# The norm between two transformer blocks: two weight panels multiplied ahead of the norm's factor

## The chip, the core and the metric

The kernel runs on one core of one Trainium2 chip. A core has five engines that run their own instruction streams and meet only at semaphores: TensorE (matmuls, PE in the profile, its weight loads PEld), VectorE (DVE), ScalarE (ACT), GpSimd (POOL) and SyncE (SP, here the queue that loads the weights). The metric is the device time of one execution in microseconds (us). Matmul results land in PSUM, which has 8 banks of 128 partitions x 512 fp32 numbers; everything else lies in SBUF.

## What is computed

Two transformer blocks of two layers each, on 512 tokens of width 1024, in fp32. Between the blocks stands a norm over the width of each token:

```python
def rmsnorm(x, g):
    y = x * rsqrt(mean(x * x, axis=-1, keepdims=True) + EPS)
    return y * g

x = first_block(...)      # ends with  return rmsnorm(x, g_final)
x = second_block(x, ...)
```

The second block's first layer multiplies the normed stream by a wide `w_in` and uses two slices of the product, `iq` (512 columns) and `iw` (8 columns), only to choose keys:

```python
proj = x @ w_in
aq, ak, av, iq, ik, iw, ... = split(proj)
# per query t and key s, over 8 index heads h:
dots  = einsum('bqhd,bsd->bqhs', iq, ik) * 64 ** -0.5
score = einsum('bqhs,bqh->bqs', relu(dots), iw * 8 ** -0.5)
# the 128 best admissible keys of each query are attended to
```

The norm's factor of token t, 1/rms(t), is positive, so that it can be taken out of `iq` (and of the relu) and put on `iw` of the same token.

## The kernel before

**Layout.** The stream lies transposed, as `X[128, 8, 512]`: tile k holds 128 of the 1024 channels for all 512 tokens. Every fp32 product is made from three: a tile is split into a high part (`XH`, rounded) and a low part (`XL`, the rest), and `wh*xh + wh*xl + wl*xh` are added up in a PSUM bank. ACT makes high parts, DVE the low parts of the stream, POOL the low parts of the weights.

**Weights.** They come as 274 panels of 1 MB through two raw buffers (`RAW`), in the order of their use. ACT's `hi(c)` (line 1246) splits panel c's high half, POOL's `low_half` (line 342) its low half, and then SP loads panel c+2 into the same raw buffer (line 330). Two panels in a row can have buffers of their own (`own_place`, `OWN_H`, `OWN_L`), so that they are split while the panels before them are still in use. The two `iq` panels of the second block's first layer have them.

**Order on TensorE.** The first block's last work is the down projection of its feed-forward part, in 8 groups. DVE adds each 128x512 result to `X` (line 2236). Then `inverse_deviation` (line 719) adds the squares of all channels up by matmuls with ones, and, once ACT has taken the root of the 4x128 sums and DVE the reciprocal, `spread` (line 709) copies the factor of each token over 128 partitions of bank 5. `keep_clock` (line 669) issues matmuls whose results nobody reads. Then `gemm_two` (line 593) multiplies the two `iq` panels: for each k ("a row" below), 8 matmuls with `XH[k]` and 4 with `XL[k]` of 384 columns, into banks 0 to 3. Behind it stands `misc`, a panel that holds `ik`, `iw` and a few others, then the panels of `aq`, and so on.

**Order on ACT.** At the end of the feed-forward part (`next_panel`, line 1495) ACT first runs five steps of `beside`, which is empty in the last layer of the first block, then splits the two `iq` panels. Behind that come `norm` (line 1539): eight squares of `X` (line 1282), the root, the `misc` panel, and eight `split_hi` of the normed stream with the next panel's split between them.

**Order on DVE.** In the last group of the down projection, `down` (line 2230) puts one step of `adding` behind each added tile from the third on: the running sum of the squares (line 1961, six additions; the last square is added on TensorE). Behind that, `norm` (line 2016): the reciprocal, then for each k a `scalar_tensor_tensor` that multiplies `X[k]` by the gain and the spread factor, in place, and the subtraction that makes `XL[k]`.

**A place of the same kind.** The first block's second layer starts differently, through `entry(1)` (ACT line 1557, DVE line 1990): its first panel is multiplied with `X` times the gain alone, and the factor comes later. There ACT makes `XH[k]` (line 1566, "u_hi") and a square in turn, DVE makes `XL[k]` from X, gain and `XH[k]` (line 1997, "u_lo") and adds a square, and TensorE makes the sums by `token_sums` (line 656; eight matmuls of one column) behind a whole panel.

Of the kernel before, what the change touches and what calls it, by code (L numbers as in the profile page):

```python
# [15 lines left out]
F32 = mybir.dt.float32  # L16
F32R = mybir.dt.float32r
I32 = mybir.dt.int32
ALU = mybir.AluOpType
# [3 lines left out]
P = 128  # L23
D = 1024
S = 512
DEPTH = 2
# [200 lines left out]
def program(nc, stream, x_in, consts_in, rot_in, vec_in, wgate_in, pos_in, out, marks):  # L227
    ctx = ExitStack()
    with ctx:
# [282 lines left out]
        def _(pe):  # L512
# [205 lines left out]

            def inverse_deviation(bank, t, l, which):

                T.after((t, l, which + "_acc", KD - 2), bank_reader[bank], own=False)
                token_columns(TMP[:, 2, :], bank, P, True, False)
                T.after((t, l, which + "_sq", KD - 1), own=False)
                T.done(token_columns(TMP[:, (KD - 1) % 2, :], bank, P, False), t, l, which + "_ms")
                bank_reader[bank] = (t, l, which + "_root")
                keep_clock(bank + 1, 1)
                spread(bank + 1, (t, l, which + "_inverse"), (t, l, which + "_spread"))
                bank_reader[bank + 1] = (t, l, which + "_scaled", KD - 1)
                keep_clock(bank, 2)
# [353 lines left out]
            inverse_deviation(4, "f", 0, "n1")  # L1083

            for l in range(DEPTH):
# [4 lines left out]
                gemm_two(w["iq"], banks, h_ready, lambda k: (t, l, "x_hi", k), lambda m: (t, l, "q", 8 + m), columns_b(8))  # L1090
# [150 lines left out]
        def _(act):  # L1241
# [159 lines left out]
            def ffn(l, t, ff, groups, kt, base_t, base_d, base_h, beside=iter(())):  # L1401
# [108 lines left out]

# [22 lines left out]
            def token_root(bank, ready, name):  # L1533

                A.after(ready)
                sums = PS[:, bank, 0:S:P] if name[0] == "f" else PS[:, bank, 0:NB]
                A.done(act.activation(ST[:, 100:104], sums, ACT.Sqrt, scale=1.0 / D, bias=ST[:, 96:97]), *name)

            def norm(t, l, which, squared, bank, second_panel, to_x=False):

                for _ in squared:
                    pass
                warm_root()
                token_root(bank, (t, l, which + "_ms"), (t, l, which + "_root"))
                hi(second_panel, used=panel_used(second_panel - 4) if to_x else None)
                for k in range(KD):
                    if to_x and k == 4:
                        hi(second_panel + 1, used=panel_used(second_panel - 3))
                    src = X[:, k, :] if to_x else TMP[:, k % 2, :]
                    hn = ("b", 0, "x_hi", k) if to_x else (t, l, ("h_hi" if which == "n1" else "h2_hi"), k)  # L1550
                    split_hi(XH[:, k, :], src, [(t, l, which + "_scaled", k)], hn, own=False)

            def read_first(l):
                for m in range(2):
                    read(("a", l, "q", m), AR[:, m, :])

# [35 lines left out]
            entries = [entry(l) for l in range(DEPTH)]  # L1592
            for l in range(DEPTH):
# [126 lines left out]
                ffn(l, t, w["ff"], FF1_GROUPS, 4, *bases(t, l), entries[l + 1] if l + 1 < DEPTH else iter(()))  # L1720
            norm("f", 0, "n1", norm_squares("f", 0, "n1", lambda k: ("a", DEPTH - 1, "ffn_out", k)), 4,
                 at_b(0)["misc"], to_x=True)
# [207 lines left out]
        def _(dve):  # L1930
# [25 lines left out]
            def sums(src, ready, name):  # L1956

                for k in range(1, KD - 1 if name[0] == "f" else KD):
# [45 lines left out]

            def scale_again(t, l, gain):
# [9 lines left out]

            def norm(t, l, which, gain, to_x=False):
                token_inverse(t, l, which)
                h = "h" if which == "n1" else "h2"
                spread_bank = 7 if which == "n2" else 5

                def dst(k):
                    return X[:, k, :] if to_x else TMP[:, k % 2, :]

                def hi_name(k):
                    return ("b", 0, "x_hi", k) if to_x else (t, l, h + "_hi", k)

                def lo_name(k):
                    return ("b", 0, "x_lo", k) if to_x else (t, l, h + "_lo", k)

                gains = VEC[:, 1 if to_x else l % 2, gain:gain + KD]  # L2030
                for k in range(KD + 1):
                    if k < KD:

                        V.after(*[hi_name(k - 2), lo_name(k - 2)] if k >= 2 else [(t, l, which + "_spread")], own=False)
                        V.done(dve.scalar_tensor_tensor(dst(k), X[:, k, :], gains[:, k:k + 1], PS[:, spread_bank, :],
                                                        ALU.mult, ALU.mult), t, l, which + "_scaled", k)
                    if k:
                        j = k - 1
                        lo(XL[:, j, :], dst(j), XH[:, j, :], [hi_name(j)], lo_name(j), own=False)
# [230 lines left out]
            entries = [entry(l) for l in range(DEPTH)]  # L2270
            for l in range(DEPTH):
# [70 lines left out]
                ffn(l, t, FF1_GROUPS, 4, *bases(t, l), entries[l + 1] if l + 1 < DEPTH else square_sums("f", 0, "n1"))  # L2342
            norm("f", 0, "n1", VB["g_final"], to_x=True)

            for l in range(DEPTH):
# [13 lines left out]
                V.after()  # L2359
                V.done(dve.memset(AR[:, 13, 0:P], 1.0))  # L2360
# [197 lines left out]
```

How the kernel before makes its waits and increments, by code:

```python
    def after(self, *names, own=True):  # L205
        need = {}
        for name in names:
            if name is None or (name not in self.marks and not self.marks.get("complete")):
                continue
            who, n = self.marks[name]
            need[who] = max(need.get(who, 0), n)
        if own:
            need[self.name] = self.n
        for who, n in need.items():
            if n > 0:
                self.eng.wait_ge(self.sems[who], n)
# [65 lines left out]
        def const_dma(eng, dst, src, name):  # L283
            if n_consts[0]:
                eng.wait_ge(const_loaded, 16 * n_consts[0])
            eng.dma_start(dst, src).then_inc(const_loaded, 16)
            n_consts[0] += 1
            marks[name] = ("const", 16 * n_consts[0])
# [27 lines left out]
        @block.sync  # L317
# [6 lines left out]
            sp.dma_start(RAW[:, 1, :], stream[1:2, :, :].rearrange("o p n -> p (o n)")).then_inc(raw_full[1], 16)
            with sp.Fori(1, NPANELS // 2) as i:
                for s in range(2):
                    sp.wait_ge(lo_ready, 2 * i + s + 1)
                    sp.dma_start(RAW[:, s, :], stream[bass.ds(2 * i + s, 1), :, :].rearrange("o p n -> p (o n)"))\
                        .then_inc(raw_full[s], 16)
            for k in range(KD):
                sp.wait_ge(sems["act"], marks.get(("b", DEPTH - 1, "ln2_x", k), ("act", 1))[1])
                sp.dma_start(out.rearrange("(k p) s -> p k s", p=P)[:, k, :], X[:, k, :]).then_inc(stored, 16)
            sp.wait_ge(stored, 16 * KD)
```

## Time and profile before

| | |
|---|---|
| time, median of the runs | 3341.56 us |
| the profiled execution's own time | 3339.35 us |
| its span, first to last instruction | 3337.5 us |
| TensorE busy (PE) | 3301.5 us, 99% of the span |
| VectorE, ScalarE, GpSimd busy | 1567.9, 1370.2, 1470.4 us |
| TensorE's granted clock, mean over the span | 0.998 of full speed |
| DMA | 299 MB, 90 GB/s mean |

The profile is of one execution. Its span is what the instructions fill; 1.8 us of its own time lie around the span. Busy shares are means over a span in which the stages have different limits, so that the stretch of the changed work has to be read by itself, in the timeline.

### The profile page before, as it was taken

Reading aid. Unit: us, or ns where it says so; the run is one execution under the profiler, and the core shown is the slowest. Engines: PE = TensorE matmul, PEld = TensorE weight load, DVE = VectorE, ACT = ScalarE, POOL = GpSimd, SP = SyncE. Lnnn points to the kernel's source line nnn. Section 1 sums busy time; section 2 is a strip of 40 time slices with the busy share of each in tenths; the row PEclk is TensorE's granted clock in tenths of the full one; section 3 lists DMA queues with packets and bytes.
Section 4 is the critical chain, followed back from the end, with each engine's and each line's share of the span. In section 5 each row is a group of like instructions: output and inputs, shape, how many; then the busy total and the mean of one; then the engine's idle time right before and its main releaser. Section 6 shows DMA issues by size and latency. Waiting matters only on the chain. (4 is left out here: it accounts for less than half of the span.)

```text
span 3337.5 us, 45362 instructions
## 1 busy us (share of the span) xinstructions
PE 3301.5 (99%) x16670; PEld 2748.5 (82%) x16670; DVE 1567.9 (47%) x2488; ACT 1370.2 (41%) x1989; POOL 1470.4 (44%) x1102
## 2 busy tenths in 40 slices
PE   9999999999999999999999999999999999999998
PEld 7888888888788888888878888888887788888887
DVE  7523332226514442224973446544488625464445
ACT  5535332224635342223364453333343635443333
POOL 4433544445343444445433345445544233445453
PEclk9999999999999999999999999999999999999999
DMA  4222222222222322222211222222222121222221
GB/s 153 89 73 86 89 103 95 94 101 95 77 76 76 103 100 100 89 101 106 88 66 66 73 92 99 84 95 101 101 81 87 64 76 68 97 85 92 101 98 66
DMA packets 44014, 299.02 MB, mean 90 GB/s; under 512 B 4816, under 2 KB 5456, under 8 KB 8784
## 3 DMA queue, kind: packets, MB, share of 16 engines
q1 hardware_dynamic: 41696, 291.52, 24.5%
q10 hardware_dynamic: 2160, 5.33, 0.5%
q8 instruction: 107, 1.75, 0.2%
q14 instruction: 51, 0.42, 0.0%
HBM read 294.74 MB, written 2.10 MB: 89 GB/s over the span
## 5 line engine op out<-in xcount | busy, mean ns | idle before, releaser
L349 POOL TENSOR_TENSOR w_lo<-w_raw,w_hi 128x512 fp32r<-128x512 f32 x1024 | 1364.6, 1365 | 1778.2 <-ACT w_hi L1257 1778.2
L526 PE MATMUL ps<-x_hi,w_hi 128*128 128x512 f32 x2296 | 907.2, 395 | 3.1 <-DVE arena L2195 2.2
L528 PE MATMUL ps<-x_hi,w_lo 128*128 128x512 f32 x2296 | 894.8, 390 | 0.0
L527 PE MATMUL ps<-x_lo,w_hi 128*128 128x512 f32 x2296 | 894.1, 389 | 0.0
L1257 ACT ACTIVATE w_hi<-w_raw 128x1024 fp32r<-128x1024 f32 x516 | 515.9, 1049 | 463.0 <-PE ps L528 339.4
L526 PEld LDWEIGHTS ps<-x_hi,w_hi 128*128 128x128 f32 x2296 | 431.5, 188 | 100.3 <-issue 6.4
L528 PEld LDWEIGHTS ps<-x_hi,w_lo 128*128 128x128 f32 x2296 | 431.2, 188 | 91.2
L527 PEld LDWEIGHTS ps<-x_lo,w_hi 128*128 128x128 f32 x2296 | 431.6, 188 | 89.0 <-issue 2.2
L526 PE MATMUL ps<-y_hi,w_hi 128*128 128x512 f32 x1056 | 411.9, 390 | 2.2 <-issue 1.9
L528 PE MATMUL ps<-y_hi,w_lo 128*128 128x512 f32 x1056 | 410.9, 389 | 0.0
L527 PE MATMUL ps<-y_lo,w_hi 128*128 128x512 f32 x1056 | 410.8, 389 | 0.0
L2236 DVE TENSOR_TENSOR x<-x,ps 128x512 f32<-128x512 f32 x272 | 182.2, 684 | 255.5 <-PE ps L528 255.3
L2195 DVE SCALAR_TENSOR_TENSOR arena<-ps,vec,arena 128x511 f32<-128x511 f32 (+1 forms) x176 | 131.5, 749 | 300.4 <-ACT arena L1467 290.1
L526 PEld LDWEIGHTS ps<-y_hi,w_hi 128*128 128x128 f32 x1056 | 198.2, 188 | 45.1 <-issue 4.2
L527 PEld LDWEIGHTS ps<-y_lo,w_hi 128*128 128x128 f32 x1056 | 198.2, 188 | 41.5 <-issue 0.5
L528 PEld LDWEIGHTS ps<-y_hi,w_lo 128*128 128x128 f32 x1056 | 198.2, 188 | 41.3
L632 PE MATMUL ps<-w_hi,x_hi 128*128 128x256 f32 x768 | 222.2, 289 | 1.2 <-POOL w_lo L349 1.2
L633 PE MATMUL ps<-w_hi,x_lo 128*128 128x256 f32 x768 | 217.1, 283 | 0.0
L634 PE MATMUL ps<-w_lo,x_hi 128*128 128x256 f32 x768 | 217.1, 283 | 0.0
L1273 ACT ACTIVATE arena<-ps 128x512 f32<-128x512 f32 x136 | 81.3, 598 | 315.8 <-PE ps L528 240.6
L1467 ACT ACTIVATE arena<-ps,vec 128x512 f32<-128x512 f32 x88 | 68.4, 779 | 277.4 <-PE ps L528 277.4
L2206 DVE SCALAR_TENSOR_TENSOR arena<-ps,tmp 128x512 f32<-128x512 f32 x64 | 44.0, 691 | 238.5 <-PE ps L528 224.9
(269 smaller groups left out, 4178.7 us busy)
## 6 DMA issues: line engine op xcount, KB each, us to landing
w_raw<-stream SPq DMA_DIRECT2D x274, 1024.0 KB, 4.8
x<-x_t SPq DMA_DIRECT2D x4, 512.0 KB, 8.1
rotary<-rot ACTq DMA_DIRECT2D x4, 512.0 KB, 4.0
y_t<-x SPq DMA_DIRECT2D x8, 256.0 KB, 2.1
ct<-consts ACTq DMA_DIRECT2D x2, 770.0 KB, 4.4
arena<-pos ACTq DMA_DIRECT2D x2, 256.0 KB, 2.6
w_gate<-w_gate_in ACTq DMA_DIRECT2D x2, 256.0 KB, 2.8
vec<-vectors ACTq DMA_DIRECT2D x4, 116.0 KB, 2.0
```

The source lines that it names most:

```text
L349: ins = nc.gpsimd.tensor_tensor(low(c)[:, o:o + S], RAW[:, c % 2, o:o + S], high(c)[:, o:o + S].bitcast(F32), ALU.subtract)
L526: pe.matmul(ps, wh, xh, start=(k == 0), stop=False)
L527: pe.matmul(ps, wh, xl, start=False, stop=False)
L528: return pe.matmul(ps, wl, xh, start=False, stop=last)
L632: pe.matmul(ps, xh, wh, start=(k == 0), stop=False)
L633: pe.matmul(ps, xl, wh, start=False, stop=False)
L634: mm = pe.matmul(ps, xh, wl, start=False, stop=(k == KD - 1))
L1257: act.activation(wh[:, o:o + 2 * S], RAW[:, s, o:o + 2 * S], ACT.Copy)\
L1273: A.done(act.activation(dst, bank_of(*name), func, **kw), *(("read",) + name))
L1467: act.activation(AR[:, j, :], PS[:, j, :], ACT.Identity, scale=VEC[:, l % 2, bass.ds(tap, 1)], bias=VEC[:, l % 2, bass.ds(bias, 1)]).then_ ...
L2195: ins = dve.scalar_tensor_tensor(AR[:, j, tap:S], PS[:, j, 0:n], wv, AR[:, j, tap:S], ALU.mult, ALU.add)
L2236: dve.tensor_tensor(X[:, m, :], X[:, m, :], PS[:, 4 + m % 4, :], ALU.add).then_inc(down_added, 1)
```

## The change

The two `iq` panels of the second block's first layer are multiplied with `X` times `g_final`, without the factor. The factor goes on `iw`. The last layer of the first block gets an `entry` of its own (`last_entry`), in which ACT makes high parts and squares in turn while the feed-forward part ends, and DVE the low parts; both `iq` panels are split ahead of these. TensorE runs two of the eight rows, then `token_sums` (now of all eight squares, which DVE adds up), a third row, `spread`, and the last five rows. `inverse_deviation` goes, and with it two calls of `keep_clock` (12 matmul instructions of 256 columns in the profile) and 16 of 128 columns. The stream is then multiplied by gain and factor as before, but each `XH[k]` is overwritten only when row k has been read, which TensorE says by a new mark.

```diff
-            def gemm_two(n, banks, ready, high_ready, name, columns):
+            def gemm_two_rows(n, banks, ready, high_ready, name, columns, read=None):
 ...
                         if k == KD - 1:
                             T.done(mm, *name(j))
+                        elif read and j == 3:
+                            T.done(mm, *read(k))
+                    if k < KD - 1:
+                        yield
...
-            inverse_deviation(4, "f", 0, "n1")
...
-                gemm_two(w["iq"], banks, h_ready, lambda k: (t, l, "x_hi", k), lambda m: (t, l, "q", 8 + m), columns_b(8))
+                if l:
+                    gemm_two(w["iq"], banks, h_ready, lambda k: (t, l, "x_hi", k), lambda m: (t, l, "q", 8 + m), columns_b(8))
+                else:
+                    index = gemm_two_rows(w["iq"], banks, lambda k: ("f", 0, "u_lo", k), lambda k: ("f", 0, "u_hi", k),
+                                          lambda m: (t, l, "q", 8 + m), columns_b(8), lambda k: ("f", 0, "u_read", k))
+                    run(index, 2)
+                    token_sums(TMP[:, 2, :], 4, ("f", 0, "n1_acc", KD - 1), ("f", 0, "n1_ms"))
+                    bank_reader[4] = ("f", 0, "n1_root")
+                    run(index)
+                    spread(5, ("f", 0, "n1_inverse"), ("f", 0, "n1_spread"))
+                    bank_reader[5] = ("f", 0, "n1_scaled", KD - 1)
+                    for _ in index:
+                        pass
...
                     else:
-                        run(beside, 5)
+                        if ff + per * groups not in own_place:
+                            run(beside, 5)
                         hi(ff + per * groups)
                         if ff + per * groups in own_place:
                             hi(ff + per * groups + 1)
+                            run(beside, 5)
...
+            def last_entry():
+                x_ready = lambda k: ("a", DEPTH - 1, "ffn_out", k)
+                squared = norm_squares("f", 0, "n1", x_ready)
+                for k in range(KD):
+                    A.after(x_ready(k), "vec%d" % (DEPTH - 1))
+                    g = VB["g_final"] + k
+                    A.done(act.activation(XH[:, k, :], X[:, k, :], ACT.Copy, scale=VEC[:, 1, g:g + 1]), "f", 0, "u_hi", k)
+                    yield
+                    if k < 6:
+                        run(squared)
+                        yield
+                for _ in squared:
+                    pass
+                warm_root()
+                token_root(4, ("f", 0, "n1_ms"), ("f", 0, "n1_root"))
...
+            misc = at_b(0)["misc"]
+            hi(misc, used=panel_used(misc - 4))
+            for k in range(KD):
+                if k == 4:
+                    hi(misc + 1, used=panel_used(misc - 3))
+                split_hi(XH[:, k, :], X[:, k, :], [("f", 0, "n1_scaled", k), ("f", 0, "u_read", k)], ("b", 0, "x_hi", k), own=False)
...
+            def last_entry():
+                adding = square_sums("f", 0, "n1")
+                for k in range(KD):
+                    g = VB["g_final"] + k
+                    V.after(("f", 0, "u_hi", k), "vec%d" % (DEPTH - 1), own=False)
+                    V.done(dve.scalar_tensor_tensor(XL[:, k, :], X[:, k, :], VEC[:, 1, g:g + 1],
+                                                    XH[:, k, :].bitcast(F32), ALU.mult, ALU.subtract), "f", 0, "u_lo", k)
+                    if k:
+                        run(adding)
+                    yield
+                for _ in adding:
+                    pass
...
+                if l == 0:
+                    V.done(dve.tensor_tensor(iw, iw, ST[:, 104:108].unsqueeze(2).broadcast_to([P, NB, 8]), ALU.mult))
+                    V.after()
```

The first `last_entry` shown is that of ACT, the second that of DVE. `scale_stream` on DVE holds the loop that `norm` held, without a change in its instructions.

## Rows read from the trace of the kernel before

**Rows 1.** The page, part 1: busy time, share of the span, instructions of each engine
```profile
PE 3301.5 (99%) x16670; PEld 2748.5 (82%) x16670; DVE 1567.9 (47%) x2488; ACT 1370.2 (41%) x1989; POOL 1470.4 (44%) x1102
```
**Rows 2.** Timeline, TensorE, around the norm: start us, us, engine, line, instruction, count
```profile
1550.28 0.39 PE L528 MATMUL ps<-y_hi,w_lo 128*128 128x512 f32 x1
1552.05 2.05 PE L679 MATMUL ps<-ct,tmp 128*128 128x128 f32 x16 [1.38 <-DVE tmp L1961]
...
1557.47 0.41 PE L531 MATMUL ps<-x_hi,own_hi 128*128 128x384 f32 x1
...
1559.63 0.33 PE L531 MATMUL ps<-x_hi,own_hi 128*128 128x384 f32 x1
...
1561.71 0.33 PE L531 MATMUL ps<-x_hi,own_hi 128*128 128x384 f32 x1
...
1574.46 0.47 PE L526 MATMUL ps<-x_hi,w_hi 128*128 128x512 f32 x1
```
**Rows 3.** Timeline, ScalarE, the same stretch
```profile
1530.92 1.99 ACT L1257 ACTIVATE own_hi<-w_raw 128x1024 fp32r<-128x1024 f32 x2
1540.11 2.01 ACT L1257 ACTIVATE own_hi<-w_raw 128x1024 fp32r<-128x1024 f32 x2 [7.21 <-DMA w_raw<-stream]
1542.03 1.34 ACT L1282 ACTIVATE tmp<-x 128x512 f32<-128x512 f32 x2
```
**Rows 4.** Timeline, GpSimd, the same stretch
```profile
1541.25 5.96 POOL L349 TENSOR_TENSOR own_lo<-w_raw,own_hi 128x512 fp32r<-128x512 f32 x4 [1.05 <-ACT own_hi L1257]
```
**Rows 5.** Timeline, VectorE, around the norm and at the end of the key selection
```profile
1537.10 0.69 DVE L2236 TENSOR_TENSOR x<-x,ps 128x512 f32<-128x512 f32 x1 [2.03 <-PE ps L528]
...
1551.31 0.68 DVE L1961 TENSOR_TENSOR tmp<-tmp 128x512 f32<-128x512 f32 x1
...
1691.05 0.29 DVE L2055 CUSTOM_DVE_ANT_0 tmp<-arena,ps 128x128 f32<-128x128 f32 x1 [4.42 <-PE ps L746]
```
**Rows 6.** Timeline, VectorE and ScalarE, entry(1) of the first block
```profile
774.19 1.18 DVE L1997 SCALAR_TENSOR_TENSOR x_lo<-x,vec,x_hi 128x512 fp32r<-128x512 f32 x1
775.48 1.60 DVE L1961 TENSOR_TENSOR tmp<-tmp 128x512 f32<-128x512 f32 x1
...
780.10 0.75 DVE L1997 SCALAR_TENSOR_TENSOR x_lo<-x,vec,x_hi 128x512 fp32r<-128x512 f32 x1
780.95 0.69 DVE L1961 TENSOR_TENSOR tmp<-tmp 128x512 f32<-128x512 f32 x1
781.56 0.68 DVE L2236 TENSOR_TENSOR x<-x,ps 128x512 f32<-128x512 f32 x1
782.16 0.74 DVE L1997 SCALAR_TENSOR_TENSOR x_lo<-x,vec,x_hi 128x512 fp32r<-128x512 f32 x1
...
774.50 0.73 ACT L1566 ACTIVATE x_hi<-x,vec 128x512 fp32r<-128x512 f32 x1
```
**Rows 7.** Timeline, TensorE, entry(1): the sums and the spread between rows of a panel
```profile
792.16 0.95 PE L660 MATMUL ps<-ct,tmp 128*128 128x1 f32 x8
792.97 0.49 PE L531 MATMUL ps<-x_hi,w_hi 128*128 128x512 f32 x1
...
795.84 1.05 PE L715 MATMUL ps<-ct,stats 128*128 128x128 f32 x8
796.64 0.48 PE L531 MATMUL ps<-x_hi,w_hi 128*128 128x512 f32 x1
```
**Rows 8.** Timeline, TensorE, an idle stretch in an attention and the matmuls behind it
```profile
832.99 1.12 PE L746 MATMUL ps<-arena 64*128 64x128 f32 x8 [2.06 <-DVE stats L2055]
834.04 0.79 PE L526 MATMUL ps<-x_hi,w_hi 128*128 128x512 f32 x1
...
836.75 0.40 PE L526 MATMUL ps<-x_hi,w_hi 128*128 128x512 f32 x1
```
**Rows 9.** Stretches: length, busy time of PE, PEld, DVE, ACT, POOL, granted clock, DMA
```profile
834.00:836.00 2.00, 2.00 (x6) 1.57 (x6) 1.32 (x9) 1.89 (x8) 1.09 (x1) 0.50 0.23 92
68.00:70.00 2.00, 0.00 (x0) 0.00 (x0) 1.79 (x10) 0.99 (x1) 0.00 (x0) 1.00 0.86 344
```

More of the change, by code:

```diff
@@ L591, in gemm_rows, with gemm_two @@
                 marks[("panel", n)] = marks[name(ms - 1)]
-            def gemm_two(n, banks, ready, high_ready, name, columns):
+            def gemm_two(*args):
+                for _ in gemm_two_rows(*args):
+                    pass
+            def gemm_two_rows(n, banks, ready, high_ready, name, columns, read=None):
                 for p in range(2):
@@ L717, in spread @@
                 T.done(mm, *name)
[L719 to L729, printed above, removed]
             def attention(pairs, l, t, fillers, ahead=0):
@@ L1089, in _ @@
                 banks = range(4) if l == 0 else range(4, 8)
-                gemm_two(w["iq"], banks, h_ready, lambda k: (t, l, "x_hi", k), lambda m: (t, l, "q", 8 + m), columns_b(8))
+                if l:
[11 more added lines that the diff above has]
+                        pass
+                    marks[("f", 0, "u_read", KD - 1)] = marks[(t, l, "q", 11)]
                 gemm(w["misc"], KD, 1, XH, XL, h_ready, lambda m: (t, l, "q", 12))
@@ L1535, in token_root, with read_first @@
                 A.after(ready)
-                sums = PS[:, bank, 0:S:P] if name[0] == "f" else PS[:, bank, 0:NB]
+                sums = PS[:, bank, 0:NB]
                 A.done(act.activation(ST[:, 100:104], sums, ACT.Sqrt, scale=1.0 / D, bias=ST[:, 96:97]), *name)
-            def norm(t, l, which, squared, bank, second_panel, to_x=False):
+            def read_first(l):
+                for m in range(2):
+                    read(("a", l, "q", m), AR[:, m, :])
+            def last_entry():
[9 more added lines that the diff above has]
+                        yield
                 for _ in squared:
@@ L1543, in norm @@
                 warm_root()
[L1544 to L1555, printed above, removed]
+                token_root(4, ("f", 0, "n1_ms"), ("f", 0, "n1_root"))
             def entry(l):
@@ L1591, in _ @@
             hi(0)
-            entries = [entry(l) for l in range(DEPTH)]
+            entries = [entry(l) for l in range(DEPTH)] + [last_entry()]
             for l in range(DEPTH):
@@ L1719, in _ @@
                     const_dma(act, VEC[:, 0, :], vec_in[2], "vec2")
-                ffn(l, t, w["ff"], FF1_GROUPS, 4, *bases(t, l), entries[l + 1] if l + 1 < DEPTH else iter(()))
-            norm("f", 0, "n1", norm_squares("f", 0, "n1", lambda k: ("a", DEPTH - 1, "ffn_out", k)), 4,
-                 at_b(0)["misc"], to_x=True)
+                ffn(l, t, w["ff"], FF1_GROUPS, 4, *bases(t, l), entries[l + 1])
+            for _ in entries[DEPTH]:
+                pass
[5 more added lines that the diff above has]
+                split_hi(XH[:, k, :], X[:, k, :], [("f", 0, "n1_scaled", k), ("f", 0, "u_read", k)], ("b", 0, "x_hi", k), own=False)
             const_dma(act, VEC[:, 1, :], vec_in[3], "vec3")
@@ L1956, in sums @@
             def sums(src, ready, name):
-                for k in range(1, KD - 1 if name[0] == "f" else KD):
+                for k in range(1, KD):
                     a = src(0) if k == 1 else TMP[:, 2, :]
@@ L2003, in entry, with scale_stream @@
                     pass
+            def last_entry():
[9 more added lines that the diff above has]
+                for _ in adding:
+                    pass
+            def scale_stream(gain):
+                for k in range(KD + 1):
+                    if k < KD:
+                        V.after(("f", 0, "n1_spread"), own=False)
+                        V.done(dve.scalar_tensor_tensor(X[:, k, :], X[:, k, :], VEC[:, 1, gain + k:gain + k + 1],
+                                                        PS[:, 5, :], ALU.mult, ALU.mult), "f", 0, "n1_scaled", k)
+                    if k:
+                        j = k - 1
+                        lo(XL[:, j, :], X[:, j, :], XH[:, j, :], [("b", 0, "x_hi", j)], ("b", 0, "x_lo", j), own=False)
             def scale_again(t, l, gain):
@@ L2014, in scale_again @@
                         lo(XL[:, j, :], TMP[:, j % 2, :], XH[:, j, :], [(t, l, "h_hi", j)], (t, l, "h_lo", j), own=False)
[L2016 to L2039, printed above, removed]
             def attention(pairs, l, t, beside):
@@ L2268, in ffn @@
                     pass
-            entries = [entry(l) for l in range(DEPTH)]
+            entries = [entry(l) for l in range(DEPTH)] + [last_entry()]
             for l in range(DEPTH):
@@ L2341, in _ @@
                 token_inverse(t, l, "n2")
-                ffn(l, t, FF1_GROUPS, 4, *bases(t, l), entries[l + 1] if l + 1 < DEPTH else square_sums("f", 0, "n1"))
-            norm("f", 0, "n1", VB["g_final"], to_x=True)
+                ffn(l, t, FF1_GROUPS, 4, *bases(t, l), entries[l + 1])
+            for _ in entries[DEPTH]:
+                pass
+            token_inverse("f", 0, "n1")
+            scale_stream(VB["g_final"])
             for l in range(DEPTH):
```

## The prediction

> **What bounds the kernel now.** Read the page's first part first: TensorE is busy 99% of the span [rows 1], so an edit can only win what TensorE loses at one place, and only if TensorE doesn't lose it again beside it. Then the timeline of TensorE around the norm [rows 2]. The last matmul of the feed-forward part starts at 1550.28. A row of the index panels, 12 matmuls of 384 columns, takes 1561.71 - 1559.63 = 2.08 us, 0.173 each, so a matmul of 512 columns takes 0.173 x 512/384 = 0.23, and TensorE is free for the next block at 1550.51. The first index matmul starts at 1557.47. Between lie 6.96 us of a wait for the sum of squares, sums, idle-time matmuls and spread. The index panels then take eight rows, 16.6 us, and `misc` starts at 1574.46; 0.35 us of these 16.99 are start and turnover. Everything that the change touches on TensorE lies between 1550.51 and 1574.46: 23.95 us. I read `misc`'s start as the goal post.
>
> Then the timelines of ScalarE, GpSimd and VectorE in the same stretch, to see when the inputs of the new order are there. ScalarE splits the first index panel at 1530.92, waits 7.21 us for the second's data, splits it from 1540.11 and is free for the stream at 1542.03 [rows 3]. GpSimd is at that panel's low half from 1541.25 to 1547.21 [rows 4]. Both panels are thus ready before 1550.51, and the first three tiles of the stream are final by 1537.10 + 0.69 [rows 5].
>
> **The change part by part.** *Rows 0 and 1 ahead of the sums.* They need u_hi and u_lo of two tiles, made from 1542.03 on, and start at 1550.51 without a wait: to 1550.51 + 2 x 2.08 = 1554.67.
>
> *The sum of squares.* This is the term that decides. `token_sums` stands behind row 1 and waits for the seventh addition, and this chain is now VectorE's whole work: u_lo of eight tiles, seven additions and the last five tiles of the stream, one behind the other. It can't start before the first u_hi, and ScalarE comes to that only behind the second panel: 1542.03 + 0.73 [rows 3, 6] and a semaphore's 0.1, so 1542.85. The steps from start to start are in entry(1) [rows 6]: u_lo to addition 0.85, addition to stream tile 0.61, stream tile to u_lo 0.60, together 2.06. u_lo 0 to the stream's tile takes 0.65; five such triples 10.3; then two pairs without a stream tile, 0.85 + 0.61 each, 2.92; and 0.08 to the end of the last: 13.95. ScalarE's u_hi and square take 1.6 us a pair with their waits [rows 3, 6] and hold u_lo 1 up by 0.3. That gives 1557.1 if nothing slows VectorE. But GpSimd works beside it until 1547.21 or a little longer, and in entry(1) beside GpSimd a u_lo took 1.18 instead of 0.75 and an addition 1.60 instead of 0.69 [rows 6]. Two u_lo and one addition fall in that time: 0.43 + 0.43 + 0.91, less part of the 0.3, gives 1558.6. If the third u_lo is caught as well, and by as much as the addition was (0.91), 1559.5. Ends: 1557.1 and 1559.5. I take 1558.5, near the middle one, whose rows are of the same instructions beside the same engine. Before, the last addition on VectorE ended at 1551.99 [rows 5], with none of the low parts in the chain.
>
> The Trainium skill (SBUF — State Buffer, "Who interferes with whom") says that a VectorE instruction with two SBUF inputs and a GpSimd instruction that reads SBUF lock each other out, one waiting for the whole of the other. Rows 6 agree with it in kind, 1.60 against 0.69. By it every such instruction up to 1547.2 could wait for one whole GpSimd instruction, a quarter of the 5.96 us [rows 4], and the chain would end about 1 us later than the upper end.
>
> *The new wait.* TensorE stands still from 1554.67 to 1558.55, 3.9 us. What is queued behind it is all its work. The removed wait was 1.38 us long [rows 2] and the matmuls around it filled the rest; nothing fills this one.
>
> *The small matmuls.* `token_sums` takes 792.97 - 792.16 = 0.81, `spread` 796.64 - 795.84 = 0.80 [rows 7], each with 0.1 for the slower first matmul behind it. The factor (root, reciprocal) is covered by row 2, 2.08 us.
>
> *The sum.* 1550.51 + 4.16 (rows 0, 1) + 3.9 (wait) + 0.9 (sums) + 2.08 (row 2) + 0.9 (spread) + 10.4 (rows 3 to 7) = 1572.85; with the turnover of 0.3, `misc` starts at 1573.1 instead of 1574.46: 1.4 us less, 2.8 at the chain's early end, 0.4 at its late end.
>
> *The clock.* Where TensorE stood idle for 2.06 us before 832.99 [rows 8], the granted clock fell: 0.50 in 834 to 836 [rows 9], which is 1.2 instead of 2.4 GHz. The six matmuls from 834.04 took 2.71 us to 836.75 instead of 6 x 0.23 = 1.4: the fall cost 1.3. In another place TensorE was idle all through 68 to 70 and kept 1.00 [rows 9]. So an idle stretch of 2 to 3 us may or may not bring the fall; 3.9 us are longer than both, and the dummy matmuls that stood here are gone. I take a fall as likely, three in four, and its price as 1.0, below the 1.3 because part of the slow time passes over the wait and over `token_sums`, which are not limited by the clock.
>
> The Trainium skill (TensorE: Matmul & The Clock Gate, "HAM oscillation — how this bites in real kernels") warns of this pattern: TensorE that idles between groups of matmuls starts each group cold. It speaks against the change; by it the sum is -0.4, by the row at 68 to 70 alone -1.4.
>
> *Moved and added work that I cost at nothing.* `misc` is split behind the root as before, but some 5 us later, at about 1560; with 5.96 us on GpSimd [rows 4] it is ready near 1567, 5 us ahead of its use, and SP's load of the panel behind it waits for this too, with as much room. The overwriting of each `XH[k]` waits for its row; only tile 7 is late: its high and low part, 0.73 + 0.75 and two waits, against 7 x 3 x 0.23 = 4.8 us that `misc` spends on the first seven tiles. The multiplication of `iw` is smaller than a stream tile's 0.68 [rows 6], and reading the index results moves behind the last high part: together VectorE is up to 2 us later against TensorE than before. VectorE comes to the end of the key selection 4.42 us before TensorE gives it work [rows 5], which covers it; without that cover it would cost those 2 us. The removed square on TensorE and the keep-clock matmuls are in the 6.96.
>
> **The sum against the runs.** The working is that of one execution, 3339.35 us (span 3337.5 and 1.8 around it). The median of the runs is 3341.56, 2.2 above. I take the difference off the median: -1.4 + 1.0 = -0.4, 3341.2.
>
> **The rivals.** *Forecast:* the wait moves to the sum of squares, 3.9 us, and the clock falls once: 3341.2, chance 0.5. Its own range is 3340.2 to 3342.2, by the chain's two ends.
> *The clock stays.* The wait is there, TensorE goes on at 2.4 GHz. For it: 68 to 70. Against it: 832.99. It gives -1.4, 3340.2; at the chain's early end -2.8, 3338.8. Chance 0.25.
> *Slower: the slow clock lasts.* Behind the wait come one-column sums, a single row, and `spread`; if these don't bring the clock back, it stays at 1.2 GHz for twice the work of rows 8 and costs 2.6. -1.4 + 2.6 = +1.2, 3342.8, and with the chain's late end 3343.8. Against it: at 832.99 the clock was back after one stretch. It decides from the point where the clock costs more than 1.4. Chance 0.18.
> *The wait goes for good.* If the sums came in time for row 1, no wait would be left: 6.96 - 0.9 - 0.9 = 5.2 less, 3336.4. The chain would have to end by 1554.67; it starts at 1542.85 and needs 13.95 us of VectorE. Chance 0.04.
> The rest, 0.03, is for what I haven't seen.
>
> **How the numbers follow.** The range holds the first three: 3338.8 to 3343.6. Faster or slower by over 2% would be 67 us, about what a measurement of this kernel can tell from no change; no case comes near: faster 0.005, same 0.985, slower 0.01.
>
> **What would show it.** Right: index matmuls from 1550.5 on without a gap behind the feed-forward part; TensorE idle for about 3.9 us before the one-column matmuls, released by VectorE's addition; rows below 1.00 of granted clock within some us of it; `misc` at 1573 to 1574. Wrong: no wait before `token_sums`; an addition chain that ends before 1557; a wait in `misc` for a low part or a panel; or VectorE not idle any more before the attention at 1691.

## The result and the profile after

The changed kernel takes 3349.5 us (median), the kernel before 3341.18: 1.0024 times as long, 95% interval 1.0016 to 1.0032, some 8 us more. It lies outside the predicted 3338.8 to 3343.6, and the interval lies wholly above 1: the change makes the kernel slower, by a quarter of a percent. One of the ten runs of the kernel before took 7672.95 us and the others 3340.89 to 3343.34; without it the median is 3341.15.

The first page of the profile doesn't show it. TensorE is busy for 3302.8 us, 3301.5 before [rows 1]; its mean clock is 0.996, 0.998 before. The 8 us have to be looked for in the stretch itself. One caution first: the feed-forward part ahead of the norm ended between 1550.4 and 1553.6 in the profiled executions, and it moved without any edit ahead of it as well (1550.51 in the kernel before, 1552.11 in e8, which is the same kernel up to there; 1552.13 after the change). So all places below are counted from the end of that part, called E.

The timeline of TensorE after the change, around the norm (start, us, engine, line, instruction):

```profile
1560.71 1.87 PE L668 MATMUL ps<-ct,tmp 128*128 128x1 f32 x8 [4.23 <-DVE tmp L1979]
1562.44 0.67 PE L531 MATMUL ps<-x_hi,own_hi 128*128 128x384 f32 x1
...
1566.02 1.05 PE L723 MATMUL ps<-ct,stats 128*128 128x128 f32 x8
1566.83 0.42 PE L531 MATMUL ps<-x_hi,own_hi 128*128 128x384 f32 x1
...
1581.63 0.47 PE L526 MATMUL ps<-x_hi,w_hi 128*128 128x512 f32 x1 [4.14 <-issue]
...
1583.52 0.63 PE L526 MATMUL ps<-x_hi,w_hi 128*128 128x512 f32 x1
1583.95 0.63 PE L527 MATMUL ps<-x_lo,w_hi 128*128 128x512 f32 x1
```

The stretches of the two falls of the clock (length, busy time of PE, PEld, DVE, ACT, POOL, granted clock, DMA):

```profile
1560.00:1566.00 6.00, 5.29 (x20) 5.29 (x21) 0.84 (x2) 2.15 (x3) 2.10 (x2) 0.54 0.00 0
1582.00:1586.00 4.00, 4.00 (x12) 3.14 (x11) 3.71 (x8) 1.10 (x3) 0.00 (x0) 0.57 0.53 215
```

These lines answer to rows 2, 7 and 8. Two rows of the index panels follow the feed-forward part without a gap. Then TensorE waits for the sum of squares, 4.23 us by the profile, which counts the tail of the last matmul as busy, and 4.42 from the end of two rows' time (1552.13 + 2 x 2.08 = 1556.29) to 1560.71. The sums take 1562.44 - 1560.71 = 1.73 us and row 2 takes 1566.02 - 1562.44 = 3.58 at a granted clock of 0.54, which is 1.2 GHz for nearly all of it. The last rows run at full speed, and `misc` stands still for 4.14 us more. The releaser of that wait is given as "issue": the profile names nobody. Behind it the clock is down again, 0.43 us from matmul to matmul instead of 0.23. `misc` starts 29.50 us behind E, 23.95 before [rows 2].

Who keeps `misc` waiting stands in ScalarE's timeline (ACTq are DMA issues):

```profile
1578.61 0.63 ACT L1284 ACTIVATE x_hi<-x 128x512 fp32r<-128x512 f32 x1 [1.07 <-DVE x L2042]
1578.62 0.34 ACTq L287 DMA_DIRECT2D vec<-vectors  x1
1580.60 0.33 ACTq L287 DMA_DIRECT2D w_gate<-w_gate_in  x1
1581.04 1.66 ACT L1767 ACTIVATE arena<-ps 128x384 f32<-128x384 f32 x3 [1.80 <-DMA vec<-vectors]
```

`misc` is summed in bank 0. Bank 0 holds the first index result, and ScalarE reads it (L1767) only behind the last high part of the stream and behind two small loads, the second of which waits for the first (`const_dma` waits for the load ahead of it). The first read is done at about 1581.6; `misc` starts at 1581.63. Before, the index results were read as soon as they were there, because ScalarE was through with the stream by then and stood waiting for TensorE:

```profile
1573.87 2.25 ACT L1749 ACTIVATE arena<-ps 128x384 f32<-128x384 f32 x4 [5.60 <-PE ps L609]
```

### The profile page after: what moved, and what is told of

The parts are those of the page before. It is cut to its first block and busy times, and to the rows that moved or that the text cites. A ratio compares the mean times of both kernels' runs of the same rounds, so it can differ in the third digit from the quotient of the medians.

```text
span 3346.9 us, 45359 instructions
## 1 busy us (share of the span) xinstructions
PE 3302.8 (99%) x16650; PEld 2749.6 (82%) x16650; DVE 1576.3 (47%) x2498; ACT 1376.2 (41%) x1997; POOL 1468.9 (44%) x1102
## 3 DMA queue, kind: packets, MB, share of 16 engines
q8 instruction: 107, 1.75, 0.2%
```

## The experiments

The terms E, "misc" and "score matmuls" (the products of `iq` and `ik`, line 1107 before, 1114 after, 1120 where the bank is edited) are as above. Theory A, B and so on are named in the expectations. Eleven kernels ran (there is no e6), each beside the kernel before on the same chip; ratios are to that. An interval is about 3 us either way, so that the times alone don't rank e1 to e7, and a difference of 1 or 2 us between two medians is not shown by them. What is said below of single microseconds rests on places in the timelines, of one profiled execution each.

**e1: the two small loads behind misc's read.**

```diff
-            const_dma(act, VEC[:, 1, :], vec_in[3], "vec3")
...
-                const_dma(act, WG[:, :], wgate_in[l], ("w_gate", l))
+                if l:
+                    const_dma(act, WG[:, :], wgate_in[l], ("w_gate", l))
...
                                    "read", t, l, "q", j)
+                            if l == 0:
+                                const_dma(act, VEC[:, 1, :], vec_in[3], "vec3")
+                                const_dma(act, WG[:, :], wgate_in[l], ("w_gate", l))
```

> The two small loads that ScalarE issues between the last high part of the stream and the reads of the index results (the next layer's vectors and the gate weights) are issued only behind the misc panel's read. Theory A (the wait of 4.1 us ahead of misc is for misc's PSUM bank, bank 0, which still holds an index result that ScalarE reads late): the read starts 1.8 us earlier, at the end of the last high part, so misc's wait falls from 4.1 to about 2.3 us and the time by 1.8 us, to about 3347.7. Theory B (misc waits for a low part of the stream or of its panel): the wait stays 4.1 and the time 3349.5. Theory C (only the slow clock costs): 3349.5 as long as the clock falls twice.

Measured: 3346.37, ratio 1.0015 (1.0006 to 1.0024). TensorE and ScalarE around `misc`, from their timelines:

```profile
1579.68 0.47 PE L526 MATMUL ps<-x_hi,w_hi 128*128 128x512 f32 x1 [2.39 <-POOL w_lo L349]
...
1578.37 0.63 ACT L1284 ACTIVATE x_hi<-x 128x512 fp32r<-128x512 f32 x1 [1.07 <-DVE x L2045]
1579.09 2.25 ACT L1770 ACTIVATE arena<-ps 128x384 f32<-128x384 f32 x4
```

The wait falls by 1.75 us, as theory A says, and the clock doesn't fall in `misc` any more (granted 1.00 from 1580 to 1590). The medians differ by 3.1 us where 1.8 were expected; the second fall, which theory A left out, was 1.6 us in the changed kernel and fits the rest. (The profile now names GpSimd as the releaser; the low half of `misc`'s panel had been done at 1568.7.)

**e2: misc in a bank of its own.**

```diff
+                if l == 0:
+                    forced.append(4)
                 gemm(w["misc"], KD, 1, XH, XL, h_ready, lambda m: (t, l, "q", 12))
```

`next_bank` takes a bank from `forced`, where there is one, instead of the ring's next.

> misc is summed in PSUM bank 4, which is free since the root was taken, instead of bank 0. Theory A: misc starts right behind the index panels; its wait of 4.1 us goes, and with it the second fall of the clock (about 1.7 us): 3343.7. Theory B: the wait for a low part or a panel stays, 3349.5. Theory C (the clock alone): the second fall goes only if the wait goes, else 3349.5.

Measured: 3346.52, ratio 1.0015 (1.0006 to 1.0024). The wait is gone to the last bit: the last four index matmuls start at 1575.35 and take 4 x 0.173 us, and `misc` starts at 1576.04.

```profile
1575.35 0.85 PE L617 MATMUL ps<-x_lo,own_hi 128*128 128x384 f32 x4
1576.04 0.39 PE L530 MATMUL ps<-x_hi,w_hi 128*128 128x512 f32 x1
```

So theory A is right on whose wait it was, and B is out. But the time fell by 3.0 us only, not by 5.8. `misc` starts 24.56 us behind E; the attention, 140.0 behind E before, starts at 145.0. TensorE's waits from 1566 to 1692 tell where the gain went (who waited for whom: us in total, times, longest):

```profile
PE ps L1120 <- ACT tmp L1756: 2.6, 5, 1.1
PE ps L644 <- POOL w_lo L349: 1.0, 1, 1.0
```

Before, the score matmuls had no such wait. ScalarE copies their results into two buffers that VectorE empties, and ScalarE's own waits ahead of these copies are for VectorE (e.g. 3.91 us at 1619.80); so behind these waits stands VectorE.

**e3: four rows ahead of the sums.** In the order on TensorE, `run(index, 2)` becomes `run(index, 4)`.

> Four rows of the index panels run ahead of the one-column sums instead of two. Theory A: the first wait (4.2 us) goes, as two rows are 4.2 us of work, and the clock stays up; but the index results are still read by ScalarE behind the last high part, which hangs on VectorE's chain behind the spread; this moves earlier only by the time that the spread does (2.3 us), so misc starts about 2.3 us earlier, behind a longer wait (8 us instead of 4): 3347.2. Theory D (the first wait costs its full length and its fall of the clock): 4.2 + 2.3 = 6.5 us less, 3343.0.

Measured: 3346.72, ratio 1.0019 (1.0010 to 1.0028).

```profile
1558.94 1.05 PE L668 MATMUL ps<-ct,tmp 128*128 128x1 f32 x8
...
1578.22 0.76 PE L526 MATMUL ps<-x_hi,w_hi 128*128 128x512 f32 x1 [8.88 <-issue]
```

The wait ahead of the sums is gone, and `misc` now waits 8.88 us instead of 4.14. It starts 27.79 us behind E, 1.7 earlier than in the changed kernel, and the median is 2.8 less. That is near theory A (2.3); D's 6.5, a ratio of 1.0005, lies outside the interval. A wait taken away on TensorE was given back at the next place where TensorE meets the same chain.

**e4: matmuls nobody reads in both waits.**

```diff
+                    keep_clock(6, 4)
                     token_sums(TMP[:, 2, :], 4, ("f", 0, "n1_acc", KD - 1), ("f", 0, "n1_ms"))
...
                     marks[("f", 0, "u_read", KD - 1)] = marks[(t, l, "q", 11)]
+                    keep_clock(6, 4)
```

> Eight matmuls nobody reads are put in each of the two waits (ahead of the one-column sums and ahead of misc), into bank 6; the waits stay as long. Theory A: each fall of the clock costs, the first 0.9 us in the one-column sums and 1.4 us in the row behind, the second 1.7 us in misc; without them 3349.5 - 4.0 = 3345.5. Theory E (the clock is a bystander, the waits alone make the loss): 3349.5. The rest up to 3341.2 would be the waits themselves.

Measured: 3345.85, ratio 1.0014 (1.0005 to 1.0023). The granted clock by stretch (columns as above):

```profile
1557.00:1566.00 9.00, 8.34 (x50) 7.48 (x50) 4.64 (x9) 4.35 (x7) 1.96 (x2) 1.00 0.00 0
1580.00:1586.00 6.00, 5.01 (x22) 4.18 (x23) 4.56 (x10) 1.97 (x4) 0.00 (x0) 1.00 0.52 209
```

With both waits filled the clock stays at 1.00, the spread starts 11.59 us behind E instead of 13.89, `misc` 27.84 instead of 29.50, and the median is 3.7 us less; 4.0 were expected. TensorE still comes to `misc` too early and has nothing of use to do, for longer than before (4.95 us from its last index matmul, 4.31 in the changed kernel), since `misc` waits for ScalarE's read. So somewhat less than half of the change's loss is the clock, the rest the waits themselves. Theory E is out by these places; by the times alone it would not be, as the two intervals overlap.

**e5: four rows and the own bank together.**

> Both waits are taken away at once: four rows ahead of the one-column sums, and misc in bank 4. Theory G (TensorE's own order sets the time): rows, sums and misc follow each other without a wait, misc starts 18.8 us behind the feed-forward part instead of 23.95, and the time is 5 us under before: 3336. Theory F (VectorE sets the time: it is at work without a break from the sums of squares over the stream's parts and the rotations to the scores, and TensorE's score matmuls wait for it): VectorE comes to the first rotation 27.5 us behind the feed-forward part, 24.07 in before; less a slack of about 1.3 us that the score matmuls had, 2.1 us over before: 3343.3, with waits in the score matmuls.

Measured: 3345.31, ratio 1.0013 (1.0003 to 1.0022). `misc` starts 18.84 us behind E, as theory G has it, 5 us earlier than before. The time is 4.4 us over before all the same. TensorE's waits behind it:

```profile
PE ps L530 <- DVE x_lo L1963: 2.3, 3, 0.8
PE ps L1120 <- DVE stats L2384: 1.8, 1, 1.8
PE ps L644 <- POOL w_lo L349: 1.0, 1, 1.0
PE ps L1120 <- ACT tmp L1756: 0.9, 2, 0.6
```

TensorE runs ahead and waits for VectorE in `misc` (the stream's low parts), ahead of the scores (the index weights), and in them. Theory G is out: TensorE's own order doesn't set the time here.

**e7: the stream's first parts between the two panels' splits.** `run(beside, 5)` stands between the two `hi` of the index panels.

> The stream's first parts are made between the splits of the two index panels instead of behind both, in ScalarE's 7.2 us of waiting for the second panel's data; nothing else of the changed kernel is touched. The chain of squares starts when the stream's tiles come and ends about 5.3 us behind the feed-forward part instead of 8.5. Theory A+F: the first wait falls from 4.2 to 1.2 us, the clock stays up there, the spread comes 4.8 us earlier and with it VectorE and the read of the index results; misc starts 24.8 us behind the feed-forward part (29.5 in the changed kernel, 23.95 in before): 3342 to 3344, by whether the clock falls in the wait ahead of misc. Theory B (misc waits for its panel, which is split behind the root): about the same gain. Theory H (the order of the splits is what made the change slow by itself): 3341 or less.

Measured: 3344.34, ratio 1.0013 (1.0004 to 1.0023). The squares end 5.68 us behind E, 8.53 in the changed kernel; the first wait is 1.39 us. `misc` starts 25.06 behind E (24.8 expected), behind a wait of 4.77 us:

```profile
1557.55 1.05 PE L668 MATMUL ps<-ct,tmp 128*128 128x1 f32 x8 [1.39 <-DVE tmp L1979]
...
1576.87 0.76 PE L526 MATMUL ps<-x_hi,w_hi 128*128 128x512 f32 x1 [4.77 <-issue]
```

It recovers 5.2 us by the medians (3.7 by the ratios) and leaves `misc`'s wait and the clock's fall in it. The order "both panels first" is one part of the loss, not the whole: theory H asked for 3341 or less, which lies outside the interval. Whether it is the dearest part the ratios don't tell (1.0013 here, 1.0013 in e5, 1.0014 in e4).

**e8: VectorE made late in the kernel before.**

```diff
+                if l == 0:
+                    for _ in range(7):
+                        V.after()
+                        V.done(dve.tensor_tensor(YSCR[:, KD + 1, :], ROT[:, 0, :], ROT[:, 1, :], ALU.add))
                 for j in range(8, 13):
                     rope_b(j)
```

> The kernel before, with seven additions of 128x512 (about 0.75 us each with their waits, 5.3 us) put on VectorE ahead of the first rotation of the index results; their result is used by nothing. Theory F: the score matmuls have about 1.3 us of slack against VectorE, the rest becomes TensorE's wait: 4.0 us more, 3345.2, waits at the score matmuls. Theory I (as the prediction had it: VectorE's lateness is covered by its wait of 4.4 us ahead of the attention): 0.9 us more, 3342.1, no waits at the score matmuls.

Measured: 3340.68, ratio 0.9999 (0.9989 to 1.0008): nothing. But it tells nothing between the theories, because I had put the additions into an idle stretch. VectorE in e8, then its waits in the kernel before (1560 to 1692):

```profile
1571.88 5.05 DVE L2356 TENSOR_TENSOR scratch<-rotary 128x512 f32<-128x512 f32 x7
1577.04 0.01 DVE L1944 LOAD_MASK_SELECT scratch<-arena  x1
```
```profile
DVE scratch L1944 <- ACT arena L1749: 4.4, 1, 4.4
DVE tmp L2055 <- PE ps L746: 4.4, 1, 4.4
```

Before, VectorE waited 4.4 us for the first index result (L1944 is the rotation), and the additions filled that. The first rotation began 24.95 us behind E instead of 24.08. What the miss is worth: it shows VectorE's slack in front of the rotations, 4.4 us, which the change had to spend as well.

**e9: all together**: the order of e7, three rows ahead of the sums, misc in bank 4, the loads of e1.

> All together: the stream's first parts between the two splits, three rows ahead of the sums, misc in bank 4, the two small loads behind misc's read. Theory G: no wait from the feed-forward part to misc, 18.5 us instead of 23.95: 5.4 us under before, 3335.8. Theory F: VectorE comes to the first rotation 23.85 us behind the feed-forward part, 0.2 earlier than in before; with the slack of 1.3 us the gain is 1.5: 3339.7, and the rest of TensorE's lead is waited off at the score matmuls.

Measured: 3343.06, ratio 1.0002 (0.9993 to 1.0012). `misc` starts 18.47 us behind E without a wait (18.5 expected), the first rotation 24.22 behind E (23.85 expected). The score matmuls wait 3.8 us, a panel 1.0, and the attention starts 141.3 us behind E, 140.0 before. Theory G's 5.4 us of gain are out. F's 1.5 can't be told from nothing by this interval; VectorE came to the first rotation nearly as F had it, but then needed 75.2 us to its last score, 72.9 before.

**e10: VectorE made late behind its idle stretch.** The same seven additions as in e8, behind the loop over the first five rotations.

> As e8, the kernel before with seven additions of 128x512 on VectorE whose result nobody uses, but now behind the first five rotations instead of ahead of them, where VectorE had 4.4 us of idle time that swallowed them. So VectorE comes 5 us late to the scores for real. Theory F (the score matmuls wait for VectorE once it is late by more than their slack, which the changed kernels put at 2 us: TensorE's last score matmul came at most 15.8 us ahead of VectorE's last score, 13.8 in before): 5.3 - 2.0 = 3.3 us more, 3344.3, with waits in the score matmuls. Theory I (hidden behind VectorE's wait ahead of the attention, 4.4 us): at most 0.9 more, 3341.9, no waits in the score matmuls.

Measured: 3345.93, ratio 1.0012 (1.0003 to 1.0022), 4.1 us more. VectorE's additions, and TensorE's waits from 1550 to 1692:

```profile
1592.14 7.94 DVE L2358 TENSOR_TENSOR scratch<-rotary 128x512 f32<-128x512 f32 x7
```
```profile
PE ps L1107 <- ACT tmp L1732: 1.9, 3, 1.1
PE ps L1107 <- DVE stats L2361: 1.9, 1, 1.9
PE ps L679 <- DVE tmp L1961: 1.4, 1, 1.4
PE ps L632 <- POOL w_lo L349: 1.0, 1, 1.0
```

They are the waits of e2, e5 and e9, made in the kernel before by late VectorE alone: GpSimd's next panel starts at the same place (42.7 us behind E in both) and takes 6.46 us, 6.38 before. VectorE's last score came 6.5 us later (103.5 us behind E, 97.0 before), TensorE's last score matmul 4.6 later (87.7 instead of 83.1): a slack of 2 us, and the rest of VectorE's delay is TensorE's too. Theory F stands; I, the prediction's view, is out by these waits (by the time only just, as its 0.9 us lie at the interval's edge). The size of the additions was off: beside GpSimd they took 7.94 us, not 5.3.

**e11: e9 with the spread as early as it can be**: `run(index, 2)`, `token_sums`, no row between, `spread`.

> As e9 (all together), but two rows ahead of the one-column sums and none between sums and spread: TensorE waits some 1.6 us for the squares and 0.7 for the factor, and the spread comes 1.9 us earlier. Theory F (VectorE from the spread on sets the time): TensorE's waits cost nothing, since it has 5 us of lead by then, VectorE starts the stream's scaling 8.4 us behind the feed-forward part instead of 10.3, and the time falls by up to 1.9 us against e9, to some 1 us under e9's ratio of 1.0002 times before, about 3340. Theory G (TensorE's order sets it): the two waits add 2.3 us to e9.

Measured: 3340.56, ratio 0.9995 (0.9986 to 1.0004). Waits of TensorE from 1550 to 1692:

```profile
PE ps L672 <- DVE tmp L1988: 1.4, 1, 1.4
PE ps L644 <- POOL w_lo L349: 1.0, 1, 1.0
PE ps L727 <- DVE stats L2015: 0.6, 1, 0.6
PE ps L1120 <- ACT tmp L1756: 0.3, 1, 0.3
```

TensorE waits 2.0 us more in the norm than in e9, and the waits in the score matmuls are down from 3.8 to 0.3. The time is not more: 0.9995 against 1.0002, with intervals that overlap. Theory G's 2.3 us on top of e9 would be 1.0009, which is out; that TensorE's waits cost nothing is as theory F has it. Against the kernel before it is no difference that can be told.

But the early spread did not bring VectorE to the rotations any earlier. The clock fell behind the two waits (granted 0.50 from 1560 to 1562), the spread took 1.73 us, and VectorE began to scale the stream 9.47 us behind E instead of 10.33: 0.9 us earlier, not 1.9. The first rotation came no earlier (24.24 behind E, 24.22 in e9), because ScalarE's last high parts waited for TensorE to read the rows that they overwrite, and VectorE for them:

```profile
1574.71 0.63 ACT L1290 ACTIVATE x_hi<-x 128x512 fp32r<-128x512 f32 x1 [1.45 <-PE ps L617]
1575.37 0.69 DVE L1966 TENSOR_TENSOR x_lo<-x,x_hi 128x512 fp32r<-128x512 f32 x1 [0.40 <-ACT x_hi L1290]
```

What differs is the stretch from there to VectorE's last score: 73.7 us, 75.2 in e9, for the same instructions. Some of them take longer beside a panel of GpSimd: in e11 the rotation's second multiplication of 128x384 (L1975) took 0.56 us at 30.45 behind E and 1.53 at 33.45, and GpSimd's panel began at 31.70. That the panels' places make the difference of 1.5 us is likely, but no run tests it.

**e12: e11 with misc's split ahead of the root.**

> As e11, and ScalarE splits the misc panel ahead of the root instead of behind it, while it waits for the one-column sums. Theory F: the panel behind comes earlier by some 3 us, so that TensorE's wait of 1.0 us for a panel's low half behind the scores goes, and GpSimd works while VectorE is idle, not beside the stream's scaling: 1 us under e11, about 3339. Theory J (GpSimd's work beside the squares slows VectorE there, or the root comes late): as e11 or up to 1 us more.

Measured: 3343.64, ratio 1.0006 (0.9997 to 1.0015). Theory J: GpSimd and ScalarE are busy with the panel while the squares end. The last addition takes 1.71 us beside GpSimd, the squares end 6.72 us behind E instead of 5.69, the first wait grows from 1.39 to 2.42 us, and the wait of 1.0 us for a panel is still there. Expected gain 1, measured loss 3 by the medians (the intervals overlap). The delay of 1.0 us at the sums becomes 2.2 at the first rotation (26.43 against 24.24 behind E), and most of the growth is the clock: behind the longer wait it is down for the sums already, so that the spread starts 9.20 us behind E instead of 7.36, and it stays down longer (granted 0.50 from 1560 to 1564, where e11 has 0.81 from 1562 to 1564), so that `misc` starts at 24.65 instead of 22.46.

**The places in one table**, worked out from the timelines, in us behind E; the first column is a difference of medians:

| kernel | time less before's | misc | VectorE: squares end | first rotation | last score | TensorE: last score matmul | attention |
|---|---|---|---|---|---|---|---|
| before | 0 | 23.95 | 1.49 | 24.08 | 96.98 | 83.14 | 140.0 |
| after | +8.3 | 29.50 | 8.53 | 29.63 | 102.88 | 90.30 | 146.7 |
| e2, own bank | +5.3 | 24.56 | 8.56 | 28.93 | 103.08 | 87.30 | 145.0 |
| e5, bank, four rows | +4.4 | 18.84 | 8.55 | 28.08 | 101.31 | 86.65 | 144.3 |
| e7, order | +3.4 | 25.06 | 5.68 | 25.19 | 97.78 | 86.57 | 143.0 |
| e9, all | +2.1 | 18.47 | 5.71 | 24.22 | 99.40 | 83.60 | 141.3 |
| e10, before, late VectorE | +4.1 | 23.95 | 1.49 | 24.08 | 103.53 | 87.73 | 145.4 |
| e11, early spread | -1.2 | 22.46 | 5.69 | 24.24 | 97.96 | 82.16 | 139.9 |

The time follows the last column, within 1.6 us, and not that of `misc`. In the kernels left out of the table the attention starts at 143.8 (e1, +5.2), 144.7 (e3, +5.5), 143.9 (e4, +4.7), 140.1 (e8, -0.3) and 142.7 (e12, +1.9). Where TensorE had waits in the score matmuls (e2, e5, e9, e10, e11), its last score matmul lies 14.7 to 15.8 us ahead of VectorE's last score: there it was held. Where it was late itself (after, e7), the distance is 11 to 13, and TensorE's own waits set the time.

## Why the prediction was wrong

**Right: the panels, the first rows, the chain.** Rows 0 and 1 started at E without a wait. I had the chain of squares end 8.0 us behind E; it ended at 1560.66, 8.53. The half microsecond is the first low part beside GpSimd, 1.58 us where I had 1.18; the steps behind it took what I had put down for them:

```profile
1544.52 1.58 DVE L2029 SCALAR_TENSOR_TENSOR x_lo<-x,vec,x_hi 128x512 fp32r<-128x512 f32 x1 [5.10 <-ACT x_hi L1559]
...
1559.97 0.69 DVE L1979 TENSOR_TENSOR tmp<-tmp 128x512 f32<-128x512 f32 x1
```

The sum of squares, named as the term that decides, thus made a wait of 4.4 us instead of 3.9.

**Mis-sized: the clock.** I took one fall for 1.0 us, and kept a longer one as a rival, at 2.6. My reason for the low price, that the one-column sums are not limited by the clock, was wrong. The first fall cost 0.9 in the sums (1.73 less 0.81) and 1.5 in row 2 (3.58 less 2.08), 2.4 in all: close to the rival, and for its reason, that one-column sums behind a wait didn't bring the clock back. The second fall, 1.6 us in `misc` (its first score matmul comes 24.07 us behind `misc` instead of 22.44), was in none of my cases, because the wait ahead of it was in none. The two falls add up to 4.0; e4, which has neither, is 3.7 faster.

**Wrong: a move costed at nothing.** The step that failed is in the part "Moved and added work that I cost at nothing". I wrote that reading the index results moves behind the last high part, and then asked only what this does to VectorE. The read also empties the PSUM bank that `misc` is summed in. I had seen the 0.35 us of "start and turnover" ahead of `misc` [rows 2] and carried it over as a constant; most of it was the end of just this wait (with a bank of its own, e2, `misc` follows the index matmuls without a gap), and it grew to 4.3 (from 1576.63 + 4 x 0.173 = 1577.32 to 1581.63). The two loads on the same queue were not priced at all, though the second waits for the first, 1.8 us.

**The working put right.** My sum gave `misc` at 22.6 behind E with the clock up. Add 0.5 of wait, 2.4 of clock and 4.0 of bank: 29.5, the measured place. That is 5.55 more than before, and 7.15 with 1.6 for the second fall. From E to the end the two profiled executions differ by 7.8 us, 0.6 more than that, which I did not follow; the medians differ by 8.3. The terms can't be taken off one by one, though: without the fall of the clock (e4) or without the first wait (e3) `misc` came only 1.7 us earlier, since its wait for the bank grew.

**Two slips in the ranges.** The forecast's early end is 3341.56 - 2.8 + 1.0 = 3339.8, not 3340.2, and the late end of the slow case, 3343.8, lies outside the 3343.6 that I let the range end at. Neither bears on a result of 3349.5.

**Wrong as well, though it didn't show: the cover.** I let VectorE's lateness go into its wait of 4.42 us ahead of the attention [rows 5]. That wait comes behind the scores, and the score matmuls need VectorE earlier, with 2 us of slack (e10). The changed kernel hid this, since TensorE itself was late. It is why neither taking away `misc`'s wait (e2) nor both waits (e5) brought the time back. The change fills TensorE's lost time at the price of eight low parts and an addition more on VectorE, 7 x 0.75 + 1.58 + 0.69 = 7.5 us (0.75 and 0.69 by [rows 6], 1.58 as above), ahead of a stretch in which VectorE had 4.4 us to spare at the rotations and 2 at the scores. So the 5 us of gain that stand in my rival "the wait goes for good" were not to be had by TensorE's order alone; e5 and e9, which have that order, show it.

The best arrangement, e11, gives the kernel before's time.

**Open.** In e2, e5, e9, e10, e11 and e12 a panel behind the scores came 1.0 us late, 0.2 before; e12 was to settle whether an earlier split of `misc` cures it, and it didn't. Nor does a run show how much of VectorE's way from the first rotation to the last score (72.6 to 75.2 us in the table's kernels without the added instructions of e10) goes by where GpSimd's panels fall.

## What to carry to other kernels

When a read of a PSUM bank moves, ask who writes that bank next, and what else stands in the reading engine's queue in front of the read. A stall on the busiest engine may be the only slack that a second, serial engine has: before filling it with that second engine's work, follow this engine to the next place where the two meet, and take the slack there, not at a later wait. Where TensorE is ahead of that meeting place, a wait taken away comes back there (e3, e5), and one put in costs nothing that could be measured (e11 against e9).

## What the runs showed of the hardware

The changed kernel's clock fell in a wait of 4.23 us and just behind one of 4.14, and behind the first it stayed at 1.2 GHz through eight one-column matmuls and nearly a whole row: 0.54 granted over 6 us. The length of the wait alone did not say when it fell. In e2 a wait of 4.26 us left the sums at full speed, 0.92 us, and the row behind them was slow, 3.73 us. Waits of 2.4 us went both ways: granted 1.00 behind 2.39 us in e1, the sums slow behind 2.42 us in e12. After 1.39 us the sums were at full speed in e7 and e11; in e7 a row followed and the clock stayed at 1.00, in e11 a second wait of 0.57 us followed and the spread was slow, 1.73 us instead of 0.8. TensorE in e2 (three lines), e11 (three) and e12 (two):

```profile
1560.10 1.06 PE L672 MATMUL ps<-ct,tmp 128*128 128x1 f32 x8 [4.26 <-DVE tmp L1985]
1561.02 0.67 PE L535 MATMUL ps<-x_hi,own_hi 128*128 128x384 f32 x1
...
1564.75 1.05 PE L727 MATMUL ps<-ct,stats 128*128 128x128 f32 x8
...
1557.73 1.05 PE L672 MATMUL ps<-ct,tmp 128*128 128x1 f32 x8 [1.39 <-DVE tmp L1988]
1559.35 2.08 PE L727 MATMUL ps<-ct,stats 128*128 128x128 f32 x8 [0.57 <-DVE stats L2015]
1561.08 0.67 PE L535 MATMUL ps<-x_hi,own_hi 128*128 128x384 f32 x1
...
1558.88 1.87 PE L672 MATMUL ps<-ct,tmp 128*128 128x1 f32 x8 [2.42 <-DVE tmp L1989]
1561.31 2.08 PE L727 MATMUL ps<-ct,stats 128*128 128x128 f32 x8 [0.57 <-DVE stats L2016]
```

Seven additions of 128x512 took 5.05 us where GpSimd was idle (e8) and 7.94 where it was at a panel for the last 5.3 us of it (e10), for the same instructions with two SBUF inputs. The Trainium skill (SBUF — State Buffer, "Who interferes with whom") states that a VectorE instruction with two SBUF inputs contends with a GpSimd instruction that reads SBUF. The trace agrees in kind, though not each addition waited for a whole instruction of GpSimd, which by [rows 4] is 1.5 us: they lost 2.9 us in seven.

Starts of the same program differ: the clock fell in the first 90 us in some profiled executions and not in others (granted 1.00 all through in the kernel before, 0.94 over the first 30 us in e8), and E moved by up to 3 us with it. A difference of 1 or 2 us between two profiles says nothing until both are counted from a place next to the edit.
